# First conv run of a streaming encoder layer: the three products of a chunk interleaved by model block, and the second chunk's mean taken from eight squares on TensorE

## The reference

```
x = x + 0.5 * swiglu_1(rms(x))
h = rms(x) * norm_mix                      # mean of squares over the 1024 of the model
u, c, b, q, k, v, f, q_mem = split(h @ w_in)
y_conv = b * causal_conv3(c * u)           # 256 channels
y_fox  = attention with forget gates(q, k, v, f)
y_mem  = attention into 256 memory tokens(q_mem)
x = x + concat(y_conv, y_fox, y_mem) @ w_out
x = x + 0.5 * swiglu_2(rms(x));  x = rms_final(x)
```

## Time and profile before

| | |
|---|---|
| median of three runs | 2166.25 us (2164.92 to 2169.3) |
| the profiled execution's own time | 2166.79 us |
| its span, first to last instruction | 2164.7 us |
| TensorE busy | 2070.7 us, 96% of the span |
| DVE, ACT, POOL busy | 61%, 41%, 15% |
| mean granted TensorE clock | 0.982 of 2.4 GHz |
| conv run 0 on TensorE | 768.5 to 814.3 us |

### The profile page before, as it was taken

The page is one execution under the profiler, slowest core; times in us unless marked ns, Lnnn a source line. Parts: engine busy times, 40 slices in busy tenths (PEclk is TensorE's granted clock), DMA queues, the critical chain, the costliest instruction groups (busy, mean ns, idle before and its releaser), DMA issues. The chain is left out here.

```text
span 2164.7 us, 37541 instructions
## 1 busy us (share of the span) xinstructions
PE 2070.7 (96%) x15160; PEld 1963.5 (91%) x15160; DVE 1311.8 (61%) x2281; ACT 886.8 (41%) x1475; POOL 334.2 (15%) x169
## 2 busy tenths in 40 slices
PE   5999999999999999999999889999999999999996
PEld 5999999999999989876877668989999999999996
DVE  7999657885331064645645555499985688733103
ACT  5445333444232131555555563154442344433213
POOL 0000000003443414011011212000000000253440
PEclk8999999999999999999999899999999999999998
DMA  6544323448542235521120134055432344674322
GB/s 220 128 137 127 100 60 116 139 120 300 178 146 88 69 110 48 87 75 45 51 75 23 49 112 173 9 166 148 133 99 77 91 139 118 205 270 161 95 69 90
DMA packets 273019, 251.57 MB, mean 116 GB/s; under 512 B 28808, under 2 KB 214792, under 8 KB 272336
## 3 DMA queue, kind: packets, MB, share of 16 engines
q1 hardware_dynamic: 272848, 249.17, 38.7%
HBM read 199.34 MB, written 49.80 MB: 115 GB/s over the span
## 5 line engine op out<-in xcount | busy, mean ns | idle before, releaser
L266 PE MATMUL banks<-hforms_hi,w_hi 128*128 128x264 f32 x2112 | 603.9, 286 | 22.6 <-DVE hforms_lo L1596 11.9
L267 PE MATMUL banks<-hforms_lo,w_hi 128*128 128x264 f32 x2112 | 602.1, 285 | 0.0
L268 PE MATMUL banks<-hforms_hi,w_lo 128*128 128x264 f32 x2112 | 599.9, 284 | 0.0
L266 PEld LDWEIGHTS banks<-hforms_hi,w_hi 128*128 128x128 f32 x2112 | 398.6, 189 | 30.7 <-issue 24.4
L836 POOL TENSOR_TENSOR w_lo<-w_raw,w_hi 128x1024 fp32r<-128x1024 f32 x88 | 219.4, 2496 | 1311.6 <-ACT w_hi L1054 1311.6
L268 PEld LDWEIGHTS banks<-hforms_hi,w_lo 128*128 128x128 f32 x2112 | 398.3, 189 | 0.0
L267 PEld LDWEIGHTS banks<-hforms_lo,w_hi 128*128 128x128 f32 x2112 | 397.5, 188 | 0.1
L268 PE MATMUL banks<-acts_a,w_lo 128*128 128x264 f32 x896 | 256.2, 286 | 0.0
L266 PE MATMUL banks<-acts_a,w_hi 128*128 128x264 f32 x896 | 254.4, 284 | 1.7 <-DVE acts_a L1624 1.7
L267 PE MATMUL banks<-acts_a,w_hi 128*128 128x264 f32 x896 | 254.9, 285 | 0.0
L1054 ACT ACTIVATE w_hi<-w_raw 128x1024 fp32r<-128x1024 f32 x88 | 93.2, 1059 | 338.1 <-PE banks L268 296.5
(11 more groups left out here) (278 smaller groups left out, 4185.5 us busy)
## 6 DMA issues: line engine op xcount, KB each, us to landing
w_raw<-in_w_ffn_down SPq DMA_DIRECT2D x88, 512.0 KB, 4.1
w_raw<-in_w_ffn_gate SPq DMA_DIRECT2D x76, 512.0 KB, 5.2
w_raw<-in_w_ffn_up SPq DMA_DIRECT2D x76, 512.0 KB, 5.2
act_rows<-act_f SPq DMA_DIRECT2D x44, 528.0 KB, 2.8
acts_f<-act_rows SPq DMA_DIRECT2D x44, 528.0 KB, 5.1
xT<-x_spill SPq DMA_DIRECT2D x3, 4224.0 KB, 16.6
w_raw<-in_w_in SPq DMA_DIRECT2D x20, 512.0 KB, 6.2
x_spill<-xT SPq DMA_DIRECT2D x4, 2112.0 KB, 8.7
```

The costliest lines, as they stand in the source:

```text
L266: eng.matmul(out, w_hi, x_hi, start=first, stop=False, skip_group_check=added)
L267: eng.matmul(out, w_hi, x_lo, start=False, stop=False, skip_group_check=added)
L268: return eng.matmul(out, w_lo, x_hi, start=False, stop=last, skip_group_check=added)
```

## The change

In run 0, the products of a chunk are no longer made one after the other. For each model block k, TensorE does the three matmuls of b = 0, then of b = 1, then of b = 2, so that the three results of a chunk are complete together. The waits that stood ahead of single products (the weights, the norm of the chunk whose mean lay in the bank, the copy that frees the bank) now all stand at the head of the chunk. After model block 5 (`MEAN_AT`) of chunk 0 comes the mean of chunk 1, after block 5 of chunk 1 the mean of chunk 2. Chunk 1 leaves `DVE_SUMS`: DVE's three additions go, its mean becomes eight matmuls from the squares, and ACT's squares of chunk 2 wait for that mean.

```diff
+        MEAN_AT = 5
+
-        DVE_SUMS = [(0, 1), (0, 1), (1,)]
+        DVE_SUMS = [(0, 1), (0,), (1,)]
...
             norm_chunk(1, 0)
-            chunk_sums(1, 1)
             norm_chunk(1, 1)
...
                 for c, (s, w) in enumerate(CHUNKS):
                     if it == 0 and c == 0:
                         pe.wait_ge(FFN["resid"], 32)
-                    if it == 0 and c == 1:
-                        norm_mean(1, 2)
+                    if it == 0:
+
+                        for b in range(3):
+                            if c == 0:
+                                pe.wait_ge(W["lo"], b + 1)
+                            if (c, b) in ((1, 2), (2, 0)):
+                                pe.wait_ge(NORM[1]["dve"], 11 * (0, 2)[c - 1] + 3)
+                            if 3 * c + b >= 8:
+                                consumed(*divmod(3 * c + b - 8, 9))
+                        for k in range(KT):
+                            for b in range(3):
+                                mm = product(cbank(0, 3 * c + b), w_slot(0, b), hh, hl, s, w, (1, c), (k,))
+                                if k == KT - 1:
+                                    mm.then_inc(CONVS["proj"], 1)
+                            if c < 2 and k == MEAN_AT:
+                                norm_mean(1, c + 1)
+                        continue
                     for b in range(3):
-                        if it == 0 and b == 1 and c == 0:
-                            norm_mean(1, 1)
                         q = 3 * c + b
                         if c == 0:
                             pe.wait_ge(W["lo"], 3 * it + b + 1)
-                        if it == 0 and q in (5, 6):
-                            pe.wait_ge(NORM[1]["dve"], 11 * (0, 2)[q - 5] + 3)
                         if 9 * it + q >= 8:
                             consumed(*divmod(9 * it + q - 8, 9))
-                        product(cbank(it, q), w_slot(it, b), hh, hl, s, w, (1, c) if it == 0 and b == 0 else None)\
-                            .then_inc(CONVS["proj"], 1)
+                        product(cbank(it, q), w_slot(it, b), hh, hl, s, w).then_inc(CONVS["proj"], 1)
```

## The result

The changed kernel takes 2181.64 us (median of 4 runs, 2180.15 to 2185.49), the kernel before 2167.74 beside it; the ratio is 1.0072, with a 95% interval of 1.0059 to 1.0084. On the profiled executions' own times it is 2181.65 against 2166.79, 14.9 us more. The forecast was 2183.8, within 2177 to 2189.

What follows compares the result with a forecast made beforehand. TensorE, busy 96%, bounds the kernel; conv run 1 follows the last h_lo by 13.6 us. That h_lo moves from 801.29 to 818.8, so 2166.8 + 17.5 = 2184.3, or 2183.8 for the median; range 2177.0 to 2189.0.

Steps and rivals of the forecast that it cites:

- The stall removed is paid away by the mean added: Chunk 0: the 1.77 us wait goes, a 4.9 us mean comes; the chunk ends at 789.0, before at 788.24.
- The half clock of 6.2 us at the start: Start of chunk 0: TensorE's clock stays at half for 6.2 us and 19 matmuls, as in the old profile.
- The wait for h_lo: Head of chunk 1: TensorE idle 4.4 us, from 789.0 until the first h_lo allows a matmul at 793.4.
- the second mean: Mean of chunk 2, behind block 5 of chunk 1: starts at 805.8 instead of 788.24 and takes 3.67 us.
- The wait for vT: Head of chunk 2: all of the chunk waits for ACT's copy until 818.6, 5.9 us idle.
- Run 1: Conv run 1 starts 13.6 us behind the last h_lo of chunk 2, at 832.4 against 814.91.
- the 17.5 forecast: Start of conv run 1: 17.5 us later than before, added to the profiled 2166.8 us.
- The lower bound: Whole change: +11.5 us, with half clock of 3.8 us, none in chunk 1, and a first mean of 2.8 us.
- No wait after 850 shrinks: Behind run 1: the prediction is wrong if a wait after 850 shrinks by several us.
- no change: Rival: slack further on absorbs the later starts, leaving 0.9 us from chunk 0, 2167.2 us; chance 0.04.
- faster: Rival: norm chain stays ahead of TensorE and mean passes cost no more than products; 5.0 us less, 2161.3; chance 0.03.
- Half clock through all of chunk 2: Rival: chunk 2 runs wholly at half clock behind the 5.9 us gap; +21.4 us, 2187.7; chance 0.07.

Runs made afterwards that it cites:

- run 0: No follow-up kernel: the first conv run inside the kernel; from its first matmul to that of run 1 46.4 us before, 59.1 changed.
- e7: Changed kernel with ACT's copy vT ahead of the norm of chunk 2 and run 1's weight loads ahead of SyncE's wait for all h_lo; ratio to before 1.0050.
- e5: Changed kernel with ACT's copy vT of the first product moved ahead of the norm of chunk 2; ratio to the kernel before 1.0067.
- e6: Changed kernel with SyncE issuing run 1's three weight loads ahead of its wait for all h_lo; ratio to the kernel before 1.0060.
- e1: Changed kernel with the mean of chunk 2 at the end of chunk 0 instead of behind block 5 of chunk 1; 2175.82 us, ratio to before 1.0034.
- e12: Kernel before with only SyncE's three weight loads of run 1 moved ahead of its wait for all h_lo; 2164.98 us, ratio 0.9990.
- e11: Changed kernel without the two conv state stores of run 1; ratio to the kernel before 1.0064.
- e8: Changed kernel with chunk 1's mean behind block 1, chunk 2's at the end of chunk 0, vT early and run 1's loads early; 2171.85 us, ratio to before 1.0004.
- e3: Kernel before, product by product, with only chunk 1's mean taken from its eight squares on TensorE, no DVE sums; 2173.61 us, ratio 1.0020.

## Why the prediction was right

The direction, the mechanism and the size held. The total came closer than its parts, in part by luck, as the last two points say:

- **Chunk 0.** "The stall removed is paid away by the mean added." The 16 passes took 781.16 - 776.30 = 4.86 us (4.9 taken, by columns from the 288-column mean). Four passes per product, as the Trainium skill has it (FP8 and Floating Point Precision, TensorE Precision Notes), would by the prediction's estimate have been 5.6; the rows stay below it. The half clock of 6.2 us at the start did not come in this execution, so the mean started 9.5 us after the first matmul and not 12.4. It did come in e7, whose mean started at 12.24: the term was right for one of the states that the same code meets.
- **Chunk 1.** The wait for h_lo was 4.22 us (4.4 forecast), by the steps named: 2.04, 1.14 and 3.93 us against 2.03, 1.14 and 3.93. Half clock behind it lasted 3.5 us, not 6.2, so the second mean started 11.0 us after the chunk and not 12.4.
- **Chunk 2.** The wait for vT was 5.72 us (5.9), the last h_lo 9.0 us behind the second mean's landing (9.0).
- **Run 1** started 12.9 us behind the last h_lo (13.6): w_raw landed 0.7 sooner after its issue.
- **The sum.** 2.9 + 1.4 + 0.7 = 5.0 us less than the 17.5 forecast make 12.5; 12.7 were measured in the stage. The mis-sized term is the half clock, for which one length, 6.2 us, the longer of the two that the rows showed, was taken twice; measured were none in chunk 0 and 3.5 us in chunk 1. The lower bound had 3.8 us in chunk 0 and none in chunk 1. That chunk 0 kept full clock was the luck of this execution.
- **What was missed:** 3.8 us behind run 1, 1.4 of them around the longer stop, 2.3 further on for a reason that stays open. "No wait after 850 shrinks" was written; that one there would grow was not thought of. By chance this made up for most of what the clock gave back, so the total, 2181.6 for a forecast of 2183.8, came closer than the stage did.

Of the rivals, "no change" and "faster" asked for the norm chain to keep ahead of TensorE or for slack further on. Neither was there: e5 and e6 show the two chains side by side, and e1 shows what it took to break them, the second mean ahead of chunk 1. Half clock through all of chunk 2 did not come; it lasted 4 us there.

## What to carry to other kernels

Before moving a small matmul to fill a gap, follow what hangs on its result: here a mean of 3.7 us was moved behind 9.5 us of products that had no need to come first, and the whole chain of the next chunk and the next run's loads moved with it. A reduction that feeds the other engines belongs as early as its input allows, even where it interrupts a dense run of products. And loads that need nothing of the chain they wait in should be issued ahead of it, though here that alone gave little: 1.7 us of the stage in e6, 0.1% in e12.

## What the runs showed that was not expected

- The same wait of 2.92 us ahead of run 0 was followed by full clock in the changed kernel, e1, e5, e6 and e11, by 5 to 6 us of half clock in the kernel before, e7 and e8, and in the other six by 1 to 2 us of full and then 3 to 4 us of half clock. Up to the first mean this is 2.8 us between e6 and e7 (9.48 against 12.24), with the same order of matmuls; single profiles must be compared with it taken out.
- TensorE's stop "issue", 61 us behind run 1, is 0.9 to 1.3 us with the old program of TensorE and 2.7 to 5.3 with each of the nine changed ones, and nothing without two stores of 1 KB each, issued some 16 us ahead of it. The nine kernels took 1.4 to 7.0 us more than the kernel before up to the store of `mix_rows` 138 us behind the start of run 1, by a stop that no dependence in the profile explains and the half clock that followed it in some. In e3 this was 3.7 of the 6.4 us that came behind run 1, while the stage itself had lost nothing.
